# First mixer: the modulation rows of groups 2 and 3 weighted and added up on GpSimd

## The chip, the core and the metric

The kernel runs on one NeuronCore of a Trainium2 chip. The metric is the device time of one execution in microseconds (us). A NeuronCore has five engines with instruction queues of their own: TensorE (PE, matrix products into PSUM banks), VectorE (DVE), ScalarE (ACT), GpSimd (POOL) and SyncE (SP, which here only issues DMAs). They are ordered among one another by semaphores alone.

## What is computed

The reference is a two-layer transformer-like model on 512 tokens of width 1024, with a second block behind it. The change lies in the first layer's conditioning and its mixer:

```python
def _adaln(cvec, w_mod, b_mod, n_chunks):
    m = jax.nn.silu(cvec) @ w_mod[:, :n_chunks * D_MODEL] + b_mod[:n_chunks * D_MODEL]
    return [m[:, None, j * D_MODEL:(j + 1) * D_MODEL] for j in range(n_chunks)]

def _even_mixer(h, p, h0):
    proj = h @ p['w_in']
    ...
    hs, h_last = _rglru(xa_raw, p, h0)
    y_a = jax.nn.gelu(gate) * (hs[0] + jnp.flip(hs[1], axis=1)).astype(h.dtype)
    u = _dwconv1d(hy, p['conv_b_w'], p['conv_b_b'])
    v, *gates = jnp.split(u, HYENA_ORDER + 1, axis=-1)
    kf = _hyena_filters_fft(h.shape[1], p)
    z = v
    for o in range(HYENA_ORDER):
        z = gates[o] * _fftconv(z, kf[:, o], p['filt_bias'][o])
    return jnp.concatenate([y_a, z], axis=-1) @ p['w_out'], h_last
```

`_adaln` is a product of one vector (1024 long) with a weight matrix of 1024 x 6144 for each layer, in float32. Each layer's result gives the shifts, scales and gates of its norms and residual additions.

## The kernel before

**Modulation rows.** The weight matrix `w_mod` is cut into rows: row n of a group g (g = n // 8, c = n % 8) is 128 of the 1024 input channels by 2048 output columns, 1 MB. Eight rows make a group; three groups make a layer. `adaln_sync` (L601) loads row n into one of the slots of a ring once row n minus the number of slots has been used. `adaln_tensor` (L616) multiplies it: four products with the 32-column stationary tile `cs[:, c, :]` (`cond`: column 0 the activated conditioning, column 1 that of the context, the rest zero), one for each 512 of the 2048 columns, into the four 32-partition strips of bank 4 or 5. The eight rows of a group accumulate there. Then DVE copies the bank to `mod_rows` (`rows_vector`, L655), PE turns it with four transposes (`turned_tensor`), and DVE adds the bias and writes `mods` (`mods_vector`, two operations). Groups 0 and 1 are used at the opening; groups 2 and 3 (rows 16 to 31) are spread over the mixer, with the two halves of the `residual` buffer as slots, which is free then; x itself is loaded into it again (`x.again`, L1270) when row 31 has been used.

**The mixer.** The input projection is 20 blocks of 128 output channels. A block is eight products 128x128 by 128x512 on PE (16 records in the trace) from a ring of two weight tiles `wring` (SP loads block n after block n-2's product). Blocks 0 to 3 go to the recurrence (RG-LRU), together with the context's; blocks 4 to 15 to the Hyena part; 16 to 19 are the gate. DVE does a depthwise convolution on each of blocks 0 to 15 straight from the bank (banks 6 and 7 in turn, so block n waits for the convolution of block n-2), and between these, unit by unit (`unit_vector`, L1074), the recurrence: 8 units (4 context, 4 main) x 2 directions, six or seven operations each over 256 or 512 elements, a scan among them. ACT does the units' sigmoids, exponentials and roots (`unit_scalar`). Then for each of two orders `o`: turns, spectra (`hyena_bins_tensor`), products with the filter's spectrum on DVE, the inverse transform (`hyena_back_tensor`), with blocks 16 to 19 between them. Last comes the output projection (`out_tensor`), whose first halves need the gated recurrence output (`gated_vector`, `ya3`), and the routing of the experts.

**Order.** Each engine's order is written out by hand in `mixer0_sync`, `mixer0_tensor`, `mixer0_vector` and `mixer0_scalar`. The rows of groups 2 and 3 are generators there: `next(rows)` issues one row. On PE they stand behind blocks 5, 7, 9, 11, 13, 14, 15 (`ROWS_BEHIND`) and between the steps of the two orders; on SP they stand behind the load of the block that `ROWS_WITH` names. GpSimd has only the experts' six indirect DMAs, from 707 us on. `Mixer` lays out SBUF by hand: `lru_slots`, `lru_tmp` and `w_more` lie in a row, and behind them begins `spare`, the buffer of the first expert weight unit.

Of the kernel before, what the change touches and what calls it, by code (L numbers as in the profile page):

```python
# [9 lines left out]
ALU = mybir.AluOpType  # L10
# [3 lines left out]
P = 128  # L14
T = 512
D = 1024
KD = D // P
# [141 lines left out]
class Kernel:  # L159
# [52 lines left out]
    def act(self, ins, name=None):  # L212

        ins.then_inc(*self.up("scalar", name))
        self.nc.scalar.wait_ge(self.sems["scalar"], self.count["scalar"])

    def mm(self, out, lhsT, rhs, start=True, stop=True):
        return self.nc.tensor.matmul(out, lhsT, rhs, start=start, stop=stop, skip_group_check=True)  # L218
# [145 lines left out]
def all_steps(stream):  # L364
    for _ in stream:
        pass
# [232 lines left out]
NEARLY = 4 * KD  # L599
# [68 lines left out]
        k.vec(v.tensor_tensor(o, turned[:, :, :, r], bias, ALU.add), f"ad.mods{g}" if r else None)  # L668


def steps_of(n):

    for _ in range(n):
        yield
# [23 lines left out]
class Mixer:  # L698
    def __init__(self, k):
        at = Place(k.nc, k.base)  # L700
        self.kf = at.sb("spectrum", [P, 2, 9, RW])
        self.gw = at.sb("lru_w", [P, 16, P])
        self.filters = Filters(at.then())
        late = at.then()
        self.fw = late.sb("dft", [P, 2, 2 * T])
        self.inv = late.sb("idft", [P, 8, T // 2])
        self.pr = late.sb("proj", [P, 20, T])
        lru = late.then()
        self.slot = lru.sb("lru_slots", [P, 2, 2, 3, T])
        more = lru.then()  # L710
        self.tmp = lru.sb("lru_tmp", [P, 2, 2, T])
        self.we = lru.sb("w_more", [P, KD, P])
        hy = late.then()
        self.sd = hy.sb("z_spectrum", [P, 2, NT, RW])
        self.zt = hy.sb("z_tm", [P, 4, RW])
        self.xz = [self.pr[:, 0:KR, :].rearrange("p c (q t) -> p c q t", q=2), more.sb("z_halves", [P, KR, 2, T // 2])]
        k.mixed = lru.next
        top = Place(k.nc, (k.nc.sbuf_usable_end - 4 * (KD * TC + TC)) // 32 * 32)
        self.xc = top.sb("ctx", [P, KD, TC])
        self.rc = top.sb("ctx_rms", [P, TC])  # L720
        self.ra = k.SQ[:, :, :].rearrange("p s (c t) -> p (s c) t", c=2)
        self.wm = k.X[:, :, :].rearrange("p (s c) t -> p s (c t)", s=2)
# [463 lines left out]
def out_sync(k, m, experts):  # L1186

    p = k.nc.sync
    for i in range(KD):
        if i == 3:  # L1190
            p.wait_ge(*k.at("cc3.mm"))
            router_sync(k, experts)
            unit_sync(k, experts, 0)
            p.wait_ge(*k.at(f"hy1.product{NT - 1}"))
            for n in range(1, NEARLIER):
                unit_sync(k, experts, n)
        p.wait_ge(*k.at(f"in{18 + i}.mm" if i < 2 else "in19.mm" if i == 2 else f"wo.mm{i - 3}"))
        p.dma_start(out_weights(k, m, i % 3), k.blocks("w_out", i)).then_inc(*k.up(f"wo{i % 3}", f"wo.w{i}", 16))


def out_half_tensor(k, m, i, q):
    for c in range(4 * q, 4 * q + 4):
        ins = k.mm(k.bank[4 + i % 4][:, :], out_weights(k, m, i % 3)[:, c, :], m.pr[:, 4 + c, :], c == 0, c == KD - 1)
    return ins


def out_tensor(k, m, experts):
    t = k.nc.tensor
    for i in range(3):
        t.wait_ge(*k.at(f"wo.w{i}"))  # L1210
        t.wait_ge(*k.at("ya3"))
        out_half_tensor(k, m, i, 0)
    t.wait_ge(*k.at(f"hy1.out{KR - 1}"))
    for i in range(KD):
        if i >= 3:
            t.wait_ge(*k.at(f"wo.w{i}"))
            if i >= 4:
                t.wait_ge(*k.at(f"wo.out{i - 4}"))
            out_half_tensor(k, m, i, 0)
        out_half_tensor(k, m, i, 1).then_inc(*k.up("tensor", f"wo.mm{i}"))  # L1220
        if i:
            route_sums_tensor(k, experts, i - 1, k.H[:, i - 1, :])
    route_sums_tensor(k, experts, KD - 1, k.H[:, KD - 1, :])
# [13 lines left out]

ROWS_BEHIND = (5, 7, 9, 11, 13, 14, 15)  # L1240
ROWS_WITH = {7: 1, 9: 1, 11: 1, 13: 1, 15: 1, 16: 1, 17: 2, 18: 1}


def mixer0_sync(k, m, experts):
    p, a = k.nc.sync, k.a
    all_steps(adaln_sync(k, m.filters.wm, 0, KD))
    rows = adaln_sync(k, m.filters.wm, KD, 2 * KD, [f"ad.row{n}" for n in (6, 7, 5)])
    for _ in range(3):
        next(rows)
    p.wait_ge(*k.at("lru.clear"))  # L1250
    p.dma_start(m.gw[0:64, :, 0:64], a["lru_w"][0]).then_inc(*k.up("lru_w0", "lru.w0", 16))
    p.dma_start(m.gw[64:128, :, 64:128], a["lru_w"][1]).then_inc(*k.up("lru_w1", "lru.w1", 16))
    block_sync(k, 0)
    block_sync(k, 1)
    all_steps(rows)
    p.wait_ge(*k.at(f"ad.row{2 * KD - 1}"))
    p.dma_start(m.fw[:, :, :], a["dft"].rearrange("p (k t) -> p k t", k=2)).then_inc(*k.up("dft", "hy.dft", 16))
    p.dma_start(m.inv[:, :, :], a["idft"].rearrange("p (k t) -> p k t", k=8)).then_inc(*k.up("idft", "hy.idft", 16))
    rows = adaln_sync(k, m.wm, 2 * KD, NEARLY)
    p.wait_ge(*k.at(f"mx.scaled{KD - 1}"))  # L1260
    next(rows)
    next(rows)
    p.dma_start(k.C[:, NFIRST:], a["consts"][:, NFIRST:]).then_inc(*k.up("consts_more", "consts.more", 16))
    for n in range(2, 20):
        block_sync(k, n)
        for _ in range(ROWS_WITH.get(n, 0)):
            next(rows)
    all_steps(rows)
    p.wait_ge(*k.at(f"ad.row{NEARLY - 1}"))
    p.dma_start(k.X[:, :, :], a["x_fm"].rearrange("p (k t) -> p k t", k=KD)).then_inc(*k.up("x_in", "x.again", 16))  # L1270
    out_sync(k, m, experts)


def mixer0_tensor(k, m, experts):
    t = k.nc.tensor
    first = adaln_tensor(k, m.filters.wm, k.cs, 0, KD, k.mrow)
    second = adaln_tensor(k, m.filters.wm, k.cs, KD, 2 * KD, k.mrow)
    opening_tensor(k, m, m.filters, first, second)
    t.wait_ge(*k.at(f"mx.shifted{KD - 1}"))
    t.wait_ge(*k.at("lru.w0"))  # L1280
    t.wait_ge(*k.at("lru.w1"))
    rows = adaln_tensor(k, m.wm, k.cs, 2 * KD, NEARLY, k.mrow)
    for n in range(KR):
        ctx_block_tensor(k, m, n)
        block_tensor(k, n, 7, f"cx.conv{n - 1}" if n else "sp.row1")
        if n == 1:
            all_steps(bins_tensor(k, m.filters, 1))
        if n:
            unit_tensor(k, m, n - 1)
        else:  # L1290
            all_steps(second)
    for n in range(KR, 16):
        block_tensor(k, n, 6 + n % 2, f"in{n - 2}.out" if n >= 6 else "cc.conv3" if n == 4 else "cx.conv3")
        if n in UNIT_AFTER:
            unit_tensor(k, m, UNIT_AFTER[n])
        if n in ROWS_BEHIND:
            next(rows)
    for o in range(2):
        hyena_turn_tensor(k, m, o)
        next(rows, None)  # L1300
        block_tensor(k, 16 + 2 * o, 6, f"in{14 + 2 * o}.out")
        next(rows, None)
        hyena_bins_tensor(k, m, o)
        next(rows, None)
        block_tensor(k, 17 + 2 * o, 7, f"in{15 + 2 * o}.out")
        next(rows, None)
        hyena_back_tensor(k, m, o)
        next(rows, None)
    out_tensor(k, m, experts)
    t.wait_ge(*k.at("consts.more"))  # L1310
    fence(k, "layer0", "tensor")


def mixer0_vector(k, m, experts):
    v = k.nc.vector
    opening_vector(k, m, m.filters)
    rows_vector(k, 1, k.mrow)
    rows = adaln_vector(k, 2 * KD, NEARLY)
    for n in range(KR):
        v.wait_ge(*k.at(f"cc{n}.mm"))  # L1320
        dwconv_vector(k, m.ra[:, n, :], k.bank[6][:, 0:TC], TC, "conv_a_w", n, KR, 4, 1, "conv_a_b", n,
# [9 lines left out]
    for n in range(KR, 16):  # L1331
        v.wait_ge(*k.at(f"in{n}.mm"))
        c = n - KR
        dwconv_vector(k, m.pr[:, 8 + c, :], k.bank[6 + n % 2][:, :], T, "conv_b_w", c, 12, 3, 1, "conv_b_b", c, f"in{n}.out")
        if c < KR:
            folded_vector(k, m, 0, c)
        for u, d in chains.get(n, ()):
            unit_vector(k, m, u, d)
        if n in ROWS_BEHIND:
            next(rows)  # L1340
    next(rows)
    next(rows)
    hyena_products_vector(k, m, 0)
    next(rows)
    next(rows)
    for c in range(KR):
        hyena_out_vector(k, m, 0, c)
        folded_vector(k, m, 1, c)
    hyena_products_vector(k, m, 1)
    all_steps(rows)  # L1350
    for c in range(KR):
        gated_vector(k, m, c)
    for c in range(KR):
        hyena_out_vector(k, m, 1, c)
    out_vector(k, m, experts)
# [82 lines left out]
def router_sync(k, m):  # L1438
    k.nc.sync.dma_start(m.rt[:, :, :], k.a["router"][m.layer].rearrange("p (k e) -> p k e", k=KD)).then_inc(
        *k.up("router", f"{m.name}.router", 16))  # L1440
# [2168 lines left out]
def build(nc, a, known):  # L3609
    k = Kernel(nc, a, known)  # L3610
# [29 lines left out]
    experts_tensor(k, experts1, both_sums)  # L3640
    second_tensor(k, second)

    for m in (experts0, experts1):
        rows_pool(k, m)

# [108 lines left out]
```

## Time and profile before

| | us |
|---|---|
| Runs (3) | 2416.41, 2422.7, 2425.77 |
| Median | 2422.7 |
| Span of the profiled execution | 2423.9 |

One execution was taken by the hardware profiler. The profile's page gives the busy time of each engine, and behind it stands the trace, from which other views are drawn: groups of instructions by line (L612 is line 612 of the kernel) and shape, instructions in order of time with the idle time before them and what ended it, tables of stretches, the DMA issues, and the chain of work that ended last, followed back from the last instruction. All times count from the span's start. An operand form such as `bank<-residual,cond 128*32 128x512` is a product of a 128x32 stationary tile with 128x512 moving elements. A float32 product shows as two records. A record's end on PE is modelled, so the distance between starts is the better measure of its cost. The first mixer takes up roughly the first 435 us of the span.

### The profile page before, as it was taken

What the parts mean: (1) busy time and instruction counts of PE and PEld (TensorE: products, weight loads), DVE (VectorE), ACT (ScalarE), POOL (GpSimd) and SP (SyncE); (2) the same over time, 40 slices, a digit from 0 to 9 for tenths busy, and PEclk for the clock granted to TensorE, in tenths of its full rate; (3) what the DMA queues carried; (4) which work ended last, traced back from release to release, by engine and by line L of the source; (5) the groups of instructions that cost most, each with busy time, mean ns of one, the idle gap of its engine ahead of it and who ended that gap; (6) DMA issues with size and microseconds to landing.
All of it is one profiled execution on the core that took longest, in us unless ns stands there. A gap on an engine that the chain in (4) does not pass through costs nothing.

```text
span 2423.9 us, 30345 instructions
## 1 busy us (share of the span) xinstructions
PE 2263.7 (93%) x12864; PEld 1173.2 (48%) x12864; DVE 988.5 (41%) x1786; ACT 489.0 (20%) x881; POOL 6.0 (0%) x10
## 2 busy tenths in 40 slices
PE   8999999799999998988899999899999999998797
PEld 2454454444443333436544433337884447776445
DVE  6568543311112115675211111136752446545574
ACT  3275000211111102022111111111113321114501
POOL 0000000000000000000000000000000000000000
PEclk9999999899999999999999999999999999999899
DMA  8513434799999994562899999962222220221051
GB/s 310 212 52 113 164 123 174 308 411 428 428 427 427 427 394 156 217 253 103 370 410 427 428 427 427 427 270 72 87 87 56 82 71 21 68 97 63 35 191 70
DMA packets 72243, 564.32 MB, mean 233 GB/s; under 512 B 10825, under 2 KB 11337, under 8 KB 39403
## 3 DMA queue, kind: packets, MB, share of 16 engines
q1 hardware_dynamic: 63648, 538.76, 55.5%
q10 hardware_dynamic: 7596, 20.47, 2.2%
q0 software_dynamic: 864, 3.15, 0.3%
q8 instruction: 102, 1.67, 0.3%
q14 instruction: 33, 0.27, 0.0%
HBM read 547.67 MB, written 14.68 MB: 232 GB/s over the span
## 4 chain that ended last, share of the span: by engine, by line
PE 74%; DVE 12%; DMA 9%; ACT 3%; issue 2%; SPq 0%; ACTq 0%; DVEq 0%
PE bank L218 72%; DMA experts<-in_exp_w 7%; DMA fast_w<-in_w_in 2%; PE bank L221 1%; DVE wring L1578 0%; DVE max L1577 0%; ACT scores_t L3370 0%; DVE residual L1735 0%; DVE fast_s L2107 0%; DVE fast_s L2110 0%; DVE fast_s L2108 0%; DVE fast_s L2109 0%; ACT wring L1673 0%; DVE squares L1703 0%; DVE residual L523 0%
## 5 line engine op out<-in xcount | busy, mean ns | idle before, releaser
L218 PE MATMUL bank<-normed,wring 128*128 128x512 f32 (+2 forms) x1120 | 460.4, 591 | 3.9 <-ACT normed L1918 2.1
L218 PE MATMUL bank<-experts,wring 128*64 128x512 f32 x1632 | 361.1, 596 | 10.1 <-DMA experts<-in_exp_w 10.1
L218 PEld LDWEIGHTS bank<-normed,wring 128*128 128x128 f32 (+1 forms) x1120 | 190.6, 184 | 232.9 <-issue 226.1
L1703 DVE TENSOR_TENSOR squares<-squares,bank 128x512 f32<-128x512 f32 x32 | 22.0, 688 | 670.5 <-ACT squares L1697 670.5
L218 PEld LDWEIGHTS bank<-experts,wring 128*64 128x64 f32 x1632 | 116.9, 137 | 247.4 <-issue 229.9
L218 PE MATMUL bank<-experts,hs_t 128*64 128x512 f32 x768 | 183.5, 598 | 9.3 <-DMA experts<-in_exp_w 8.9
L218 PE MATMUL bank<-rms,y 128*128 128x512 f32 x256 | 125.5, 609 | 6.0 <-ACT y L1829 2.7
L1735 DVE SCALAR_TENSOR_TENSOR residual<-bank,mods,residual 128x512 f32<-128x512 f32 x128 | 96.1, 751 | 74.1 <-PE bank L218 67.4
L218 PEld LDWEIGHTS bank<-experts,hs_t 128*64 128x64 f32 x768 | 61.4, 138 | 124.7 <-issue 122.8
L1697 ACT ACTIVATE squares<-bank 128x512 f32<-128x512 f32 x32 | 19.1, 598 | 469.9 <-PE bank L218 469.9
L218 PE MATMUL bank<-proj 64*64 64x64 f32 (+1 forms) x2192 | 94.0, 233 | 5.8 <-ACT proj L2927 4.8
L218 PEld LDWEIGHTS bank<-proj 64*64 64x64 f32 (+1 forms) x2192 | 77.5, 139 | 16.4 <-issue 5.6
L1673 ACT ACTIVATE wring<-bank,mods,gains 128x128 f32<-128x128 f32 x128 | 58.6, 458 | 103.7 <-PE bank L218 90.9
L218 PE MATMUL bank<-fast_t,fast_s 128*128 128x256 f32 x336 | 74.8, 379 | 0.0
L218 PE MATMUL bank<-proj,wring 128*128 128x512 f32 (+1 forms) x168 | 69.3, 565 | 5.5 <-DVE proj L1362 3.9
L218 PE MATMUL bank<-normed,hs_t 128*64 128x512 f32 x160 | 70.5, 594 | 1.8 <-ACT wring L1673 0.9
L218 PEld LDWEIGHTS bank<-rms,y 128*128 128x128 f32 x256 | 42.8, 190 | 52.7 <-DVE residual L1735 25.9
L218 PEld LDWEIGHTS bank<-fast_t,fast_s 128*128 128x128 f32 x336 | 63.8, 190 | 8.7
L218 PE MATMUL bank<-normed,fast_w 128*128 128x256 f32 (+1 forms) x256 | 66.7, 406 | 0.0
L218 PEld LDWEIGHTS bank<-pick,h_tm 128*128 128x128 f32 x512 | 59.4, 192 | 5.7 <-issue 4.3
L1829 ACT COPY y<-bank 128x512 f32<-128x512 f32 x32 | 18.8, 586 | 211.7 <-PE bank L218 211.2
L218 PE MATMUL bank<-pick,h_tm 128*128 128x128 f32 x512 | 59.8, 275 | 0.0
(616 smaller groups left out, 2756.0 us busy)
## 6 DMA issues: line engine op xcount, KB each, us to landing
experts<-in_exp_w SPq DMA_DIRECT2D x146, 2048.0 KB, 22.4
spare<-in_exp_w SPq DMA_DIRECT2D x20, 2048.0 KB, 22.7
normed<-in_exp_w SPq DMA_DIRECT2D x20, 2048.0 KB, 23.3
wring<-in_w_in SPq DMA_DIRECT2D x44, 512.0 KB, 3.6
wmod<-in_w_mod SPq DMA_DIRECT2D x16, 1024.0 KB, 5.9
residual<-in_w_mod SPq DMA_DIRECT2D x16, 1024.0 KB, 6.3
cf_wmod<-in_w_mod SPq DMA_DIRECT2D x16, 1024.0 KB, 5.7
fast_w<-in_w_in SPq DMA_DIRECT2D x30, 512.0 KB, 4.3
```

Source lines behind the costliest of these rows:

```text
L218: return self.nc.tensor.matmul(out, lhsT, rhs, start=start, stop=stop, skip_group_check=True)
L221: return self.nc.tensor.transpose(out, in_, self.con("ident", 0, n, 0, n))
L1673: k.act(k.nc.scalar.activation(m.xs[:, c, :], k.bank[6 + h][:, (c % 4) * P:(c % 4 + 1) * P], ACT.Identity, bias=k.MOD[:, m.layer, 24 + c, ...
L1697: k.act(k.nc.scalar.activation(m.hs[:, e, :], k.bank[2 - 2 * e][:, :], ACT.Silu), f"{m.name}.silu{i}.{e}")
L1703: k.vec(v.tensor_tensor(m.hs[:, e, :], m.hs[:, e, :], k.bank[3 - 2 * e][:, :], ALU.mult), f"{m.name}.hs{i}.{e}")
L1735: k.vec(v.scalar_tensor_tensor(out=k.X[:, c, :], in0=k.bank[4 + c % 2][:, :], scalar=k.MOD[:, m.layer, 40 + c, 0:1], in1=k.X[:, c, :], op0 ...
L1829: k.act(s.copy(m.yy[:, 512 * f:512 * f + 512], k.bank[f][:, :]), f"{m.name}.yy{i}.{f}")
```

## The change

On GpSimd a new function, `summed_pool`, takes each row of groups 2 and 3 as it lands: it multiplies the 128x2048 row with its channel's conditioning (column 0 of `cond`, one scalar for each partition) in place and adds it to an accumulator `mod_sums`; the first row of a group is multiplied straight into it. When a group's eight rows are in, PE multiplies the accumulator once with a 128x32 tile of ones (four products, one for each strip), which adds up over the partitions, and the copy, the turns and the addition of the bias follow as before. The bias is added for column 0 only (`gain_mods_vector`). The sums and turns of group 2 stand behind blocks 10 and 12, those of group 3 behind blocks 18 and 19, and the gate products on DVE now stand before the addition of group 3's bias. SP issues one row with each of blocks 2 to 9 and 12 to 17. The accumulator takes 8 KB a partition where `spare` begins, so SP waits for the sums of group 3 before the first expert unit. The output projection waits for `ad.mods3`, since it writes bank 5.

```diff
@@ class Kernel
+    def pool(self, ins, name=None):
+        ins.then_inc(*self.up("pool", name))
+        self.nc.gpsimd.wait_ge(self.sems["pool"], self.count["pool"])
@@ new functions
+def summed_pool(k, m, lo, hi):
+    p = k.nc.gpsimd
+    for n in range(lo, hi):
+        g, c = n // KD, n % KD
+        w, scale = m.wm[:, (n - lo) % 2, :], k.cs[:, c, 0:1]
+        p.wait_ge(*k.at(f"ad.w{n}"))
+        if c == 0:
+            p.wait_ge(*k.at(f"ad.sums{g - 1}" if n > lo else "cond"))
+            k.pool(p.tensor_scalar(m.acc[:, :], w, scale, None, ALU.mult), f"ad.row{n}")
+        else:
+            k.pool(p.tensor_scalar(w, w, scale, None, ALU.mult))
+            k.pool(p.tensor_tensor(m.acc[:, :], m.acc[:, :], w, ALU.add), f"ad.row{n}")
+
+def sums_tensor(k, m, g):
+    t = k.nc.tensor
+    t.wait_ge(*k.at(f"ad.row{KD * g + KD - 1}"))
+    t.wait_ge(*k.at(f"ad.mods{g - 2}"))
+    for q in range(4):
+        ins = k.mm(k.bank[4 + g % 2][32 * q:32 * q + 32, :], k.con("ones", 0, 32), m.acc[:, 512 * q:512 * q + 512])
+    ins.then_inc(*k.up("tensor", f"ad.sums{g}"))
+
+def sums_vector(k, g, rows):
+    k.nc.vector.wait_ge(*k.at(f"ad.sums{g}"))
+    k.vec(k.nc.vector.tensor_copy(rows[:, :], k.bank[4 + g % 2][:, :]), f"ad.rows{g}")
+
+def gain_mods_vector(k, g):
...
+    k.vec(v.tensor_tensor(o, turned[:, :, :, 0], bias, ALU.add), f"ad.mods{g}")
@@ class Mixer
         hy = late.then()
+        self.acc = lru.then().sb("mod_sums", [P, 2048])
@@ def out_sync
             router_sync(k, experts)
+            p.wait_ge(*k.at(f"ad.sums{NEARLY // KD - 1}"))
             unit_sync(k, experts, 0)
@@ def out_tensor
         t.wait_ge(*k.at("ya3"))
+        t.wait_ge(*k.at("ad.mods3"))
         out_half_tensor(k, m, i, 0)
@@
-ROWS_BEHIND = (5, 7, 9, 11, 13, 14, 15)
-ROWS_WITH = {7: 1, 9: 1, 11: 1, 13: 1, 15: 1, 16: 1, 17: 2, 18: 1}
+ROWS_WITH = (*range(2, 10), *range(12, 18))
@@ def mixer0_sync
         block_sync(k, n)
-        for _ in range(ROWS_WITH.get(n, 0)):
+        if n in ROWS_WITH:
             next(rows)
-    all_steps(rows)
@@ def mixer0_tensor
-    rows = adaln_tensor(k, m.wm, k.cs, 2 * KD, NEARLY, k.mrow)
...
-        if n in ROWS_BEHIND:
-            next(rows)
+        if n == 10:
+            sums_tensor(k, m, 2)
+        if n == 12:
+            turned_tensor(k, 2, k.mrow)
     for o in range(2):
         hyena_turn_tensor(k, m, o)
-        next(rows, None)
         block_tensor(k, 16 + 2 * o, 6, f"in{14 + 2 * o}.out")
-        next(rows, None)
+        if o:
+            sums_tensor(k, m, 3)
         hyena_bins_tensor(k, m, o)
-        next(rows, None)
         block_tensor(k, 17 + 2 * o, 7, f"in{15 + 2 * o}.out")
-        next(rows, None)
+        if o:
+            turned_tensor(k, 3, k.mrow)
         hyena_back_tensor(k, m, o)
-        next(rows, None)
@@ def mixer0_vector
-        if n in ROWS_BEHIND:
-            next(rows)
-    next(rows)
-    next(rows)
+        if n == 11:
+            sums_vector(k, 2, k.mrow)
+        if n == 13:
+            gain_mods_vector(k, 2)
     hyena_products_vector(k, m, 0)
-    next(rows)
-    next(rows)
...
     hyena_products_vector(k, m, 1)
-    all_steps(rows)
+    sums_vector(k, 3, k.mrow)
     for c in range(KR):
         gated_vector(k, m, c)
+    gain_mods_vector(k, 3)
@@ def build
+    summed_pool(k, mixer0, 2 * KD, NEARLY)
     for m in (experts0, experts1):
         rows_pool(k, m)
```

## Rows read from the trace of the kernel before

**Rows 1.** The page, part 1: busy time, share of the span and instructions of each engine.

```profile
PE 2263.7 (93%) x12864; PEld 1173.2 (48%) x12864; DVE 988.5 (41%) x1786; ACT 489.0 (20%) x881; POOL 6.0 (0%) x10
```

**Rows 2.** Table of stretches; columns named in its first line.

```profile
core 0: us, PE busy (x) PEld busy (x) DVE busy (x) ACT busy (x) POOL busy (x), PEclk, DMA share, GB/s
...
172.00:261.00 89.00, 89.00 (x252) 36.69 (x251) 70.97 (x105) 42.99 (x52) 0.00 (x0) 1.00 0.37 128
261.00:370.00 109.00, 99.53 (x361) 53.16 (x359) 51.98 (x88) 9.85 (x15) 0.00 (x0) 0.98 0.40 155
```

**Rows 3.** Chain of work that ended last, 90 to 520 us: start, length, what.

```profile
128.00 132.07 PE bank L218 x376
...
283.49 16.42 PE bank L218 x56
...
369.27 0.70 DVE proj L1362
...
370.11 62.91 PE bank L218 x226
```

**Rows 4.** PE in order of time, 168 to 392 us; then the rows' products by tile.

```profile
191.24 1.07 PE L218 MATMUL bank<-residual,cond 128*32 128x512 f32 x8
192.24 7.13 PE L218 MATMUL bank<-normed,wring 128*128 128x512 f32 x16
...
310.18 1.06 PE L218 MATMUL bank<-residual,cond 128*32 128x512 f32 x8
313.54 2.79 PE L221 MATMUL bank<-consts,z_halves 128*128 128x128 f32 x16 [2.29 <-DVE proj L1176]
...
318.03 0.66 PE L221 MATMUL bank<-consts,mod_rows 128*128 128x128 f32 x4
...
365.62 0.60 PE L221 MATMUL bank<-consts,mod_rows 128*128 128x128 f32 x4
...
L218 PE MATMUL bank<-residual,cond x128: 592/617/1059, 172.9 to 351.2; 128*32 128x512 f32 x128
```

**Rows 5.** Groups of instructions by line and shape, DVE, 140 to 262 us.

```profile
L559 DVE SCALAR_TENSOR_TENSOR proj<-bank,vecs,proj 128x511 f32<-128x511 f32 x28 | 21.0, 750 | 1.0
L554 DVE TENSOR_SCALAR proj<-bank,vecs 128x512 f32<-128x512 f32 x14 | 11.3, 810 | 20.2 <-PE bank L218 20.0
...
L1084 DVE TENSOR_TENSOR lru_slots<-lru_slots 128x512 f32<-128x512 f32 x8 | 5.5, 692 | 0.3
L1089 DVE TENSOR_TENSOR_SCAN lru_slots<-lru_slots,lru_state 128x512 f32<-128x512 f32 x4 | 5.1, 1284 | 0.1
...
L1082 DVE TENSOR_SCALAR lru_slots<-lru_slots 128x512 f32<-128x512 f32 x8 | 3.4, 427 | 0.3
...
L1084 DVE TENSOR_TENSOR lru_slots<-lru_slots 128x256 f32<-128x256 f32 x8 | 3.4, 425 | 0.3
...
L1089 DVE TENSOR_TENSOR_SCAN lru_slots<-lru_slots 128x256 f32<-128x256 f32 x4 | 2.8, 691 | 0.1
L1082 DVE TENSOR_SCALAR lru_slots<-lru_slots 128x256 f32<-128x256 f32 x8 | 2.4, 294 | 0.3
```

**Rows 6.** Instructions in order of time, DVE, 250 to 280 us.

```profile
259.19 0.81 DVE L554 TENSOR_SCALAR proj<-bank,vecs 128x512 f32<-128x512 f32 x1 [5.67 <-PE bank L218]
...
274.77 0.69 DVE L1147 TENSOR_TENSOR squares<-bank,spectrum 128x512 f32<-128x512 f32 x1 [10.97 <-PE bank L218]
...
276.22 0.69 DVE L1149 TENSOR_TENSOR z_spectrum<-squares 128x512 f32<-128x512 f32 x1
```

**Rows 7.** Groups of instructions by line, POOL, whole span (the memsets' other three are alike).

```profile
L1650 POOL DMA_INDIRECT h_tm<-token_rows,place x6 | 5.8, 959 | 1511.7 <-DVE gate L1624 1302.9 <-DVE gate L1622 208.8
L3750 POOL MEMSET const-uint8-127<- 128x1 uint8 x1 | 0.1, 118 | 0.0
```

**Rows 8.** DMA issues, 80 to 520 us (last number: median us to landing); SP's timeline.

```profile
residual<-in_w_mod SPq DMA_DIRECT2D x16, 1024.0 KB, 6.3
...
351.83 0.33 SPq L1270 DMA_DIRECT2D residual<-in_x_fm  x1
```

More of the change, by code:

```diff
@@ L668, in mods_vector @@
         k.vec(v.tensor_tensor(o, turned[:, :, :, r], bias, ALU.add), f"ad.mods{g}" if r else None)
+def summed_pool(k, m, lo, hi):
[21 more added lines that the diff above has]
+def gain_mods_vector(k, g):
+    v, layer, i = k.nc.vector, g // 3, g % 3
+    v.wait_ge(*k.at(f"ad.turned{g}"))
+    turned = k.bank[4 + g % 2][:, :].rearrange("p (j q r) -> p q j r", q=4, r=32)
+    bias = k.vector_of("b_mod", 48 * layer + 16 * i, 16).rearrange("p (q j) -> p q j", q=4)
+    o = k.MOD[:, layer, 16 * i:16 * i + 16, 0].rearrange("p (q j) -> p q j", q=4)
+    k.vec(v.tensor_tensor(o, turned[:, :, :, 0], bias, ALU.add), f"ad.mods{g}")
 def steps_of(n):
@@ L1317, in mixer0_vector @@
     rows_vector(k, 1, k.mrow)
-    rows = adaln_vector(k, 2 * KD, NEARLY)
     for n in range(KR):
```

## Prediction

> **What bounds the kernel now.** I read the page first. TensorE (PE) is busy for 93% of the span, VectorE (DVE) for 41%, GpSimd (POOL) for 6.0 us in all [rows 1]. The edit touches one stage only, the first mixer from 88 to 370 us, so the averages say little, and the second view is the table of stretches. From 172 to 261 us PE is busy for 89.00 of 89 us at full clock, and DVE for 70.97 us; from 261 to 370 us PE has 9.5 us of idle time [rows 2]. The third is the chain of work that ended last. It runs on PE without a break from 128.00 to 260.1 us, later for 16.42 us up to 299.9, and ends the stage with DVE's four gate products, the last at 369.27 us, after which PE goes on at 370.11 [rows 3]. So a microsecond of PE work taken out before 261 us shortens the kernel, as long as DVE, which is busy for 80% there, still keeps up. PE has two banks for the blocks, and block n waits for DVE's convolution of block n-2.
>
> **What is removed from TensorE.** A row is four column groups, and its eight records together take 1.07 us; the next block starts 1.00 us after the row (191.24 to 192.24) [rows 4]. I count 1.0 us for each. The record says 16 rows x 8 = 128 [rows 4]. Nine rows lie before the spectra of order 0 at 271 us: 9.0 us, less 1.0 for the new sums of group 2 (four products of the same shape as a row) and 0.6 for its four turns, moved here from 318.03 us, where they took 0.66 [rows 4]: 7.4 us gained. Of the seven others, the two behind the spectra and block 17 give 2.0. The one at 310.18 gives nothing: PE then waits until 313.54 for DVE in any case [rows 4]. The next, with the turns of group 2 behind it at 318.03, gives 1.0 + 0.6 = 1.6. The one behind block 18 is replaced by the sums of group 3: 0. The last two give 2.0 less 0.6 for the turns of group 3, moved ahead of the inverse transform: 1.4. The sum so far is 7.4 + 2.0 + 1.6 + 1.4 = 12.4 us.
>
> **What moves at the end of the stage.** Now the turns (0.60 us) come behind the inverse transform, then DVE's two additions and four gate products, and PE stands still from 366.22 to 370.11, 3.89 us, before the output projection [rows 3, 4]. Afterwards the gate products wait only for block 19's activation and lie beside the 14 us inverse transform, and the last turns are over before it. PE goes on at once: 0.6 + 3.9 = 4.5 us gained. What is late next there is DVE's second output step, which now begins with the first finished column chunk instead of at 370 us; three half projections of 3.5 us each (half a block's 7.0) lie before PE needs it, so nothing of the 4.5 comes back. The new wait for `ad.mods3` in front of the projection is the last of those short DVE operations and is met. Altogether TensorE's side gives 12.4 + 4.5 = 16.9 us, taken as 17. Everything behind (router, experts' weight loads) starts from events of this stage and shifts with it.
>
> **What is added to GpSimd.** There are 2 + 14 x 2 = 30 instructions over 128x2048 floats. The trace has no arithmetic on POOL, only four memsets of 128x1 at about 0.1 us and six indirect DMAs [rows 7], so both ends come from DVE. A two-input operation there takes 425 ns for 256 elements and 692 for 512, 1.04 ns an element; for 2048 that is 0.69 + 1536 x 1.04 ns = 2.3 us. The scan takes 2.31 ns an element (1284 - 692 over 256), 4.8 us for 2048. One input in SBUF takes 294 and 427 ns, 0.52 ns an element: 1.2 us, or 2.4 us without that double rate [rows 5]. I take 4.5 us for the addition, two operands fetched one after the other at DVE's pace of 1.04 ns, plus issue, near the upper end, and 2.0 for the scaling: 6.5 us a row, 3.5 to 7.2. The Trainium skill (GPSIMD Engine Reference, 3.1 Elementwise) gives 4497 ns for that addition; no trace here shows it.
>
> **Its schedule.** A row lands 6.3 us after its issue [rows 8]. Each buffer is used in turn, so two rows take at least 6.3 + 6.5 = 12.8 us, 6.4 a row, and GpSimd's own time is 6.5, against 7.0 us for a bare block [rows 4] and about 8.5 with what stands behind it (blocks 8 to 15 take 68 us, from 191.24 to 259.2 [rows 4, 6]). GpSimd keeps up: group 2 is added up by about 183 us, and its sums stand behind block 10 at about 215. Row 24 must wait for these sums, since there is one accumulator, and from there rows follow block by block until about 268 us; the sums of group 3 are wanted at about 312. On SP's queue each row's wait now stands in front of the next weight block. Row n-2 is done before that block may be fetched, so at 6.5 us it costs nothing. The copy of x, the output weights and the experts' first units stand behind row 31 as they did (x at 351.83 [rows 8]); they go out earlier. The wait for `ad.sums3` ahead of unit 0 is met by order, being behind block 19's product. DVE loses two small additions. Behind GpSimd's rows only the experts' indirect DMAs are queued, which come long after [rows 7].
>
> **What it may cost DVE.** This decides. From 140 to 262 us DVE runs the recurrence: its operations take two tensors from SBUF (692 ns for 512 elements). The spectra products show the same 0.69 us with one operand from PSUM as with both from SBUF, and one SBUF input runs at twice the rate of a PSUM one, 427 against 810 ns [rows 5, 6]. So DVE draws on SBUF over two read paths at once. The question is whether GpSimd comes in over one of these. Bounds: nothing, or DVE's two-input operations stand for the whole GpSimd instruction. I take the upper end, because DVE's rows need both paths in full and leave no cycle to share. Rows 16 to 19 are done before 140 us, where DVE has little to do. Rows 20 to 30, eleven of them, fall beside the recurrence. In each DVE loses 6.5 us less what it can do with one SBUF operand. That is the convolution, 0.81 + 2 x 0.75 = 2.3 us [rows 5], beside every second row: 1.2. So 11 x 5.3 = 58 us. DVE's idle time in front of the block convolutions is 20 us in this stretch [rows 5], 5.67 of it at 259.19 us [rows 6]. 58 - 20 = 38 us come through to PE, which stands at blocks 7, 8 and 12 to 16 for a convolution that DVE has not reached. Net: -17 + 38 = +21 us. PE's new idle time may also lower its clock; the stretch that has such idle time is at 0.98 [rows 2], about 2 us in 109, and it stays out.
>
> What the rows show is two read paths; that GpSimd sits on one of them they can't. The Trainium skill says so (SBUF: State Buffer, Practical consequences): a Vector instruction with two SBUF inputs contends with a GpSimd instruction that reads SBUF, and the pair is held for a whole instruction. By that rule it is the +21 us sum, without it the -17 us one. Its advice for such a pair is to schedule whichever is off the critical path, which speaks against this change, where the lent engine takes the path of a busy one.
>
> **The rivals.** (a) GpSimd reads beside DVE at no cost. For it: nothing in the trace shows a conflict, and there are sixteen rows with ample slack before either sum is wanted. Against: the two read paths above. Mechanism and place: fewer than the 20 us of DVE's idle time are lost, that is under 1.8 us a row, and the 14 products and the 3.9 us wait go. Time: 2422.7 - 17 = 2406; it decides for faster. (b) They share path by path: DVE goes at half speed for the 11 x 6.5 = 71 us, loses 35, 20 of it idle: -17 + 15 = -2 us, 2421. (c) The path is free but GpSimd is slower than all rows suggest, say 13 us a row. Against 8.5 us a block that is 4.5 too slow, and behind rows 26 to 29 SP holds back four blocks' weights: 4 x 4.5 = 18 us, -17 + 18 = +1 us, 2424; it begins to cost at 8.5 us a row.
>
> **How the numbers follow.** The profiled span is 2423.9 us and the median of the runs 2422.7, 1.2 less, so I add to the median: 2422.7 + 21 = 2444. The likeliest case's own range comes from the price of a row: with 3.5 us, 11 x 2.3 = 25, less 20, is 5, giving -12; with 7.2 us and nothing done beside it, 79 - 20 - 17 = +42: 2411 to 2465. Chances: blocking 0.50 (0.46 slower, 0.04 within), free 0.34 (0.31 faster, 0.03 within), shared 0.11 (within), slow GpSimd 0.05 (within). About 0.5%, 12 us, is what a measurement can tell from no change. Faster 0.31, same 0.23, slower 0.46. The range takes in (a): 2404 to 2462.
>
> **What would show it.** In the profile after: 30 POOL instructions, near 2.0 and 4.5 us. Blocking shows in DVE's recurrence operations: some of 692 ns stretched to several us while POOL is busy, and PE idle in front of blocks, released by DVE's convolution. If these stay at 692 ns, (a) holds, and PE's stretch to 261 us ends 8 us sooner with no gaps. Under (c) PE waits for the block weights' DMA. The gain at 366 to 370 us should be there in every case. I am wrong if DVE is barely slowed, or if GpSimd's rows fall mostly where DVE idles.

## The result and the profile after

The changed kernel is slower: 2464.4 us as the median of its runs (2461.2 to 2466.4), against 2422.3 for the kernel before in the same comparison. The ratio is 1.0175, 95% interval 1.016 to 1.019, which is +42 us. The forecast was slower, at +21 us, and its range ended at 2462. The profiled execution has a span of 2459.9 us, 36.0 more than that of before; it is the shortest of its runs.

The page of the changed kernel, part 1, beside [rows 1]:

```profile
PE 2246.5 (91%) x12752; PEld 1170.9 (48%) x12752; DVE 1059.0 (43%) x1784; ACT 488.7 (20%) x881; POOL 158.6 (6%) x40
```

TensorE is busy for 17 us less. The work taken out is 112 records, about 15 us at 1.07 us for eight [rows 4]; the rest mixes in other differences, among them blocks that run slower behind a wait (below). VectorE has 70.5 us more, although two of its instructions fewer are in the list (1784 against 1786), and GpSimd went from 6.0 to 158.6 us. DVE has been given no work: its instructions take longer. The table of stretches, beside [rows 2] (the same columns):

```profile
core 0: us, PE busy (x) PEld busy (x) DVE busy (x) ACT busy (x) POOL busy (x), PEclk, DMA share, GB/s
...
172.00:261.00 89.00, 69.37 (x163) 29.68 (x161) 85.27 (x94) 51.22 (x65) 39.13 (x8) 0.91 0.29 100
261.00:330.00 69.00, 41.36 (x100) 19.14 (x100) 57.79 (x39) 4.22 (x6) 58.32 (x12) 0.79 0.31 107
```

PE, which had filled 172 to 261 us without a gap, is busy for 69.37 of these 89 us; DVE is busy for 85.27 instead of 70.97. They have changed places. GpSimd's groups by line, beside [rows 7]:

```profile
L688 POOL TENSOR_SCALAR residual<-residual,cond 128x2048 f32<-128x2048 f32 x14 | 77.7, 5553 | 31.9 <-DMA residual<-in_w_mod 31.0
L689 POOL TENSOR_TENSOR mod_sums<-mod_sums,residual 128x2048 f32<-128x2048 f32 x14 | 63.9, 4563 | 1.2
```

The addition took 4.56 us on average (I had taken 4.5), the weighting 5.55 (I had taken 2.0). PE in order of time, with what ended its idle time in brackets, beside [rows 4]:

```profile
158.04 9.80 PE L223 MATMUL bank<-normed,wring 128*128 128x512 f32 x16 [6.44 <-DVE squares L564]
...
200.99 5.38 PE L223 MATMUL bank<-proj,lru_w 128*128 128x512 f32 x8 [14.26 <-DVE lru_slots L1128]
...
280.54 1.08 PE L226 MATMUL bank<-consts,mod_rows 128*128 128x128 f32 x4 [24.92 <-DVE mod_rows L704]
...
310.54 8.65 PE L223 MATMUL bank<-normed,wring 128*128 128x512 f32 x16 [4.16 <-DVE proj L564]
...
330.56 8.83 PE L223 MATMUL bank<-z_tm,dft 128*128 128x512 f32 x16 [4.51 <-DVE z_spectrum L1199]
...
396.47 13.98 PE L223 MATMUL bank<-idft,z_spectrum 128*128 128x256 f32 x64
410.29 7.03 PE L223 MATMUL bank<-proj,wring 128*128 128x512 f32 x16
```

In the kernel before PE was busy without a gap from 128.00 us until the products of order 0. Now it stands still for 6.44, 14.26, 24.92 and 4.16 us, each time for DVE, and for 4.51 us between the spectra of order 0, where it was 1.04. Only the 6.44 and the 4.16 us lie in front of a block (4 and 16). The 14.26 us lie in front of the products of a recurrence unit, and the 24.92 us between block 12 and the turns of group 2, which wait for DVE's copy. The end of the stage is as predicted: the output projection at 410.29 follows the inverse transform (396.47 + 13.98 = 410.45, its end being modelled) with no gap, where there were 3.89 us.

### The profile page after: what moved, and what is told of

It is laid out like the page before. It is cut to its first block, busy times and chain, and to the rows that moved or that the text cites. A ratio compares the mean times of both kernels' runs of the same rounds, so it can differ in the third digit from the quotient of the medians.

```text
span 2459.9 us, 30167 instructions
## 1 busy us (share of the span) xinstructions
PE 2246.5 (91%) x12752; PEld 1170.9 (48%) x12752; DVE 1059.0 (43%) x1784; ACT 488.7 (20%) x881; POOL 158.6 (6%) x40
## 4 chain that ended last, share of the span: by engine, by line
PE 69%; DVE 17%; DMA 9%; ACT 3%; issue 2%; ACTq 0%; SPq 0%; DVEq 0%
PE bank L223 67%; DMA experts<-in_exp_w 6%; DMA fast_w<-in_w_in 2%; PE bank L226 1%; DVE lru_slots L1130 1%; DMA ctx<-in_ctx_fm 1%; DVE proj L564 1%; DVE lru_slots L1131 1%; DVE lru_slots L1129 1%; DVE lru_slots L1128 1%; DVE wring L1623 0%; DVE lru_slots L1127 0%; DVE max L1622 0%; ACT scores_t L3415 0%; DVE residual L1780 0%
## 5 line engine op out<-in xcount | busy, mean ns | idle before, releaser
L223 PE MATMUL bank<-normed,wring 128*128 128x512 f32 (+2 forms) x1120 | 466.0, 598 | 14.5 <-DVE squares L564 6.4
L1695 POOL DMA_INDIRECT h_tm<-token_rows,place x6 | 5.8, 971 | 1221.2 <-PE bank L223 597.7
L688 POOL TENSOR_SCALAR residual<-residual,cond 128x2048 f32<-128x2048 f32 x14 | 77.7, 5553 | 31.9 <-DMA residual<-in_w_mod 31.0
L223 PE MATMUL bank<-normed,hs_t 128*64 128x512 f32 x160 | 70.5, 594 | 1.8 <-ACT wring L1718 0.9
L689 POOL TENSOR_TENSOR mod_sums<-mod_sums,residual 128x2048 f32<-128x2048 f32 x14 | 63.9, 4563 | 1.2
```

What stands on the lines that cost most here:

```text
L688: k.pool(p.tensor_scalar(w, w, scale, None, ALU.mult))
L689: k.pool(p.tensor_tensor(m.acc[:, :], m.acc[:, :], w, ALU.add), f"ad.row{n}")
```

## The mechanism, instruction by instruction

Two stretches of the changed kernel side by side, GpSimd first, then DVE. They are lined up by their starts:

```profile
241.92 5.56 POOL L686 TENSOR_SCALAR mod_sums<-residual,cond 128x2048 f32<-128x2048 f32 x1 [47.31 <-PE bank L223]
247.57 5.48 POOL L688 TENSOR_SCALAR residual<-residual,cond 128x2048 f32<-128x2048 f32 x1
...
264.15 4.54 POOL L689 TENSOR_TENSOR mod_sums<-mod_sums,residual 128x2048 f32<-128x2048 f32 x1
...
241.48 0.69 DVE L1128 SCALAR_TENSOR_TENSOR lru_slots<-lru_tmp,lru_slots 128x512 f32<-128x512 f32 x1
242.21 5.55 DVE L1129 TENSOR_SCALAR lru_slots<-lru_slots 128x512 f32<-128x512 f32 x1
247.80 4.08 DVE L1130 TENSOR_TENSOR lru_slots<-lru_slots,proj 128x512 f32<-128x512 f32 x1
251.91 0.69 DVE L1131 TENSOR_TENSOR lru_slots<-lru_slots 128x512 f32<-128x512 f32 x1
...
264.38 4.86 DVE L1130 TENSOR_TENSOR lru_slots<-lru_slots,proj 128x512 f32<-128x512 f32 x1
```

DVE's `TENSOR_SCALAR` at 242.21, SBUF to SBUF, took 0.43 us before [rows 5]; it now takes 5.55 and ends at 247.76. Less its own 0.43 that is 247.33, just when GpSimd's weighting ends (241.92 + 5.56 = 247.48). The next weighting begins at 247.57, and DVE's `TENSOR_TENSOR` with two operands in SBUF (0.69 us before) takes 4.08: less its own 0.69 it was let go at 251.19. The one at 251.91 takes 0.69 again, though GpSimd's instruction lasts until 253.05. So a two-input operation is held for the first 3.6 us of a weighting of 5.48, one at the double rate for all of it. In this trace eight two-input operations meet a weighting in its first part, and all are let go 3.6 to 3.9 us after its recorded start. Beside an addition (264.15 to 268.69) the two-input operation takes 4.86 us; less its own 0.69 that is 268.55, the addition's end. The operation just ahead at 241.48 lasts 0.69 us as ever, though GpSimd began within it: it was already on its way. All convolution steps, with one operand in a bank and one in SBUF, keep their 750 ns:

```profile
L1130 DVE TENSOR_TENSOR lru_slots<-lru_slots,proj 128x512 f32<-128x512 f32 x8 | 17.3, 2158 | 0.3
L564 DVE SCALAR_TENSOR_TENSOR proj<-bank,vecs,proj 128x511 f32<-128x511 f32 x23 | 17.2, 750 | 0.8
...
L1129 DVE TENSOR_SCALAR lru_slots<-lru_slots 128x512 f32<-128x512 f32 x8 | 9.8, 1228 | 0.3
```

(Groups of DVE by line and shape, 140 to 300 us, beside [rows 5].) The Trainium skill (SBUF — State Buffer, Who interferes with whom, Practical consequences) has this rule: VectorE with two SBUF inputs contends with a GpSimd instruction that reads SBUF, and with any GpSimd instruction when it runs in a 2-port mode, as the double-rate operations would. The traces agree in who waits and who doesn't. In how long they differ for one case: its summary says that the second one blocks until the first finishes, and here a two-input operation is let through after 3.6 of the weighting's 5.48 us. Why, no run here shows.

## Experiments

### The order alone, without GpSimd's work

```diff
-            k.pool(p.tensor_scalar(m.acc[:, :], w, scale, None, ALU.mult), f"ad.row{n}")
+            k.pool(p.memset(m.acc[:, :], 0.0), f"ad.row{n}")
         else:
-            k.pool(p.tensor_scalar(w, w, scale, None, ALU.mult))
-            k.pool(p.tensor_tensor(m.acc[:, :], m.acc[:, :], w, ALU.add), f"ad.row{n}")
+            k.pool(p.tensor_scalar(w[:, 0:1], w[:, 0:1], scale, None, ALU.mult))
+            k.pool(p.tensor_tensor(m.acc[:, 0:1], m.acc[:, 0:1], w[:, 0:1], ALU.add), f"ad.row{n}")
```

> The changed kernel in all its order and waits, but GpSimd's work is left out: the accumulator is set to 0 once a group, and of each later row only one column of 2048 is weighted and added, so the sums of groups 2 and 3 aren't computed. Theory A (DVE is held up by GpSimd's instructions): PE's side of the change alone is left, 17 us under the kernel before, about 2406 us, and DVE's recurrence operations are back at 692 ns. Theory B (the new order, with PE's sums and turns waiting for DVE's copy in the middle of the recurrence, and the gate products moved, costs the time by itself): it stays above the kernel before, 2430 us or more. Theory C (GpSimd too slow for SP's queue) also gives 2406.

Measured: 2402.3 us, ratio 0.9932 (0.9913 to 0.9951), which is -16.5 us (interval -21 to -12). The edit's gain on TensorE, -17 by the forecast, is there, and the order, the waits and the place of the turns cost nothing while DVE keeps up. Between 125 and 269 us PE waits for DVE once, 1.91 us ahead of the turns of group 2. Theory B falls. DVE is busy for 989.6 us:

```profile
PE 2237.8 (93%) x12752; PEld 1169.3 (49%) x12752; DVE 989.6 (41%) x1784; ACT 488.9 (20%) x881; POOL 21.1 (1%) x40
```

(page of this kernel, part 1). So GpSimd's work costs 42.4 + 16.5 = 59 us (each term known to about 4 us), and it stretches DVE's instructions by 1059.0 - 989.6 = 69.4 us.

### Weighting alone and addition alone

```diff
-            k.pool(p.tensor_tensor(m.acc[:, :], m.acc[:, :], w, ALU.add), f"ad.row{n}")
+            k.pool(p.tensor_tensor(m.acc[:, 0:1], m.acc[:, 0:1], w[:, 0:1], ALU.add), f"ad.row{n}")
```

> The changed kernel with the weighting of all 16 rows in full (5.5 us each), but the addition only in one column of 2048, so the sums are incomplete. Theory A: DVE is held up by the weighting alone, 11 rows x (4.1 - 1.2) = 32 us, 20 of them idle time that DVE has, less 17: -5 us, about 2417 us; DVE operations are stretched by up to about 4 us. Theory C (SP's queue held back by 10.1 us a row): at 5.5 us a row nothing is held back, 2406 us, and DVE's operations stay at 692 ns.

Measured: 2427.0 us, ratio 1.0025 (1.0011 to 1.0040), +6 us; DVE is busy for 1019.9 us, 30.3 more than in e1_no_pool_work. The other way round, the weighting of rows 1 to 7 of a group cut down to one column and the addition in full:

> The changed kernel with the addition of rows in full (4.5 us each), the weighting of rows 1 to 7 of a group only in one column of 2048, so the sums are those of unweighted rows. Theory A: 11 x (4.5 - 1.2) = 36 us, less 20 idle, less 17: about -1 us, 2421 us. Theory C: 2406 us. If the addition (two operands read) holds DVE up and the weighting (one operand) doesn't, this one is near 2440 and the weighting alone near 2406.

Measured: 2431.9 us, ratio 1.0048 (1.0033 to 1.0063), +12 us; DVE is busy for 1022.2 us, 32.6 more. Theory C wanted 2406 from both and falls: at 4.7 or 5.5 us a row nothing is held back on SP's queue, and both still lose the gain. Either instruction holds DVE up, with one operand read from SBUF as with two. Both came out 10 us above my estimate; I had let 20 us of the loss fall into idle time. From e1_no_pool_work's -16.5 they have lost 22.6 and 28.1 us, so only 30.3 - 22.6 = 8 and 32.6 - 28.1 = 5 us were hidden.

### Busy, but only writing

```diff
-            k.pool(p.tensor_scalar(w, w, scale, None, ALU.mult))
+            for _ in range(5):
+                k.pool(p.memset(w, 0.0))
```

with the addition cut down to one column and the first row replaced by a fill, as in e1_no_pool_work.

> The changed kernel, in which GpSimd fills each landed row with zeros five times (a fill of 128x2048 took 1.81 us in e1_no_pool_work, so about 9 us a row and 10 with the small operations) instead of weighting and adding it; the sums are not computed. GpSimd is as busy as in the changed kernel (10.1 us a row) but reads nothing large from SBUF. Theory A1 (the read path is what is held): DVE's operations stay at 692 ns, and the time is 2402 us as in e1_no_pool_work. Theory A2 (writing holds DVE up as well): near 2460 us. Theory C (a slow GpSimd holds back the block weights on SP's queue): PE waits for DMAs of weights, 10.1 - 8.5 = 1.6 us for each of four to six blocks, 2406 to 2412 us, with DVE's operations at 692 ns.

Measured: 2403.1 us, ratio 0.9925 (0.9897 to 0.9953), although GpSimd is busy for 140.4 us. Its groups and then those of DVE, by line and shape:

```profile
L689 POOL MEMSET residual<- 128x2048 f32 x70 | 126.8, 1811 | 25.4 <-DMA residual<-in_w_mod 21.5
...
L1130 DVE TENSOR_SCALAR lru_slots<-lru_slots 128x256 f32<-128x256 f32 x8 | 7.5, 931 | 0.3
L1130 DVE TENSOR_SCALAR lru_slots<-lru_slots 128x512 f32<-128x512 f32 x8 | 6.7, 836 | 0.3
...
L1132 DVE TENSOR_TENSOR lru_slots<-lru_slots 128x512 f32<-128x512 f32 x8 | 5.5, 692 | 0.3
```

This kernel separates three things that the changed kernel has together. A GpSimd that is only busy costs nothing that shows. Nor does a row that takes 9.3 us before SP can go on: PE waits for the DMA of a weight block once, for 0.33 us. In the changed kernel, whose rows take 10.1 us, none of PE's waits between 128 and 410 us is for a DMA, so theory C falls. And writes don't hold up a two-input operation (692 ns). They do hold up the double-rate ones: 931 and 836 ns on average where it was 294 and 427, DVE busy by 7.1 us more, which its idle time hid. So it is GpSimd's reading that costs here.

### The price of the weighting

```diff
-            k.pool(p.tensor_scalar(w, w, scale, None, ALU.mult))
+            k.pool(p.tensor_scalar(w, w, 0.5, None, ALU.mult))
```

> The changed kernel with the weighting by a constant 0.5 instead of the per-partition scalar read from SBUF (the sums are therefore others). If the per-partition scalar makes the weighting cost 5.5 us instead of the 2.0 that I took, it falls to about 2 us and the time to about 2445 us, where I had predicted it. If the float32 scaling costs 5.5 us with either, the time stays at 2464 us.

Measured once: 2464.7 us. The group by line on GpSimd:

```profile
L688 POOL TENSOR_SCALAR residual<-residual 128x2048 f32<-128x2048 f32 x14 | 76.6, 5471 | 30.0 <-DMA residual<-in_w_mod 29.2
```

5.47 us, so the scalar operand isn't what makes it dear. Scaling 2048 floats in place costs GpSimd more than adding two such rows (4.5 us). Why, no run here shows.

### Where the turns stand

```diff
-        if n == 12:
+        if n == 15:
             turned_tensor(k, 2, k.mrow)
```

> The changed kernel with the turns of group 2 behind block 15 instead of block 12, and the addition of its bias behind the products of order 0. In the changed kernel PE stood still for 24.92 us in front of these turns. Theory A (DVE is the bound throughout the recurrence, and the wait only shows where PE meets it): the wait goes to the blocks behind, and the time stays within 5 us of 2464 us. Theory B (the position of the turns makes a wait of its own, since DVE copies the sums only behind a recurrence unit): 10 to 20 us less, 2444 to 2454 us.

Measured: 2467.1 us, ratio 1.019 (1.015 to 1.023), from two runs 13 us apart. PE in order of time, beside the changed kernel's 24.92 us in one piece:

```profile
256.32 7.11 PE L223 MATMUL bank<-normed,wring 128*128 128x512 f32 x16 [0.86 <-DVE proj L564]
282.81 8.88 PE L223 MATMUL bank<-normed,wring 128*128 128x512 f32 x16 [19.39 <-DVE proj L564]
298.02 9.80 PE L223 MATMUL bank<-normed,wring 128*128 128x512 f32 x16 [6.33 <-DVE proj L564]
...
316.30 9.20 PE L223 MATMUL bank<-normed,wring 128*128 128x512 f32 x16 [6.29 <-DVE proj L564]
```

The wait has broken up into 0.86, 19.39, 6.33 and 6.29 us ahead of blocks 13 to 16, each for a convolution: 32.9 us, where the changed kernel has 24.92 + 4.16 = 29.1 in this part. The gain of 10 to 20 us that theory B wanted is outside the interval. The turns only mark the point where PE met DVE; whether their place is worth a few us, two runs can't tell.

### Does the lower clock cost anything?

Behind its waits PE is slow: block 4 took 9.80 us where 7.03 is usual, and the stretch from 261 to 330 us has a granted clock of 0.79, a mean between the levels of 2.4 and 1.2 GHz. I counted about 10 us of longer blocks and formed theory D, that they are part of the 42. The test fills the waits with idle work:

```diff
+def warm_tensor(k, m, count):
+    for _ in range(count):
+        k.mm(k.bank[5][:, :], m.gw[:, 0, :], m.gw[:, 4:8, :].rearrange("p a b -> p (a b)"))
```

> The changed kernel with 53 products into a bank that nobody reads, put where PE stood still in it: 6 ahead of block 4, 14 behind block 6, 25 ahead of the turns of group 2, 4 behind the first turns and 4 ahead of the third spectrum of order 0, about 0.88 us each, no more in each place than the wait there. DVE's delays stay. Theory D (behind each wait PE works at a lower granted clock: block 4 took 9.80 us for 7.03, and the stretch 261 to 330 us was at 0.79): the slow stretches go, and it is up to 10 us faster than the changed kernel, about 2454 to 2458 us. If the clock cost nothing that counts, since DVE bounds the stretch anyway, it stays at 2464 us; if the products delay PE, it is above 2466 us.

Measured: 2466.3 us, ratio 1.0174 (1.0145 to 1.0203). The stretches:

```profile
125.00:172.00 47.00, 44.98 (x137) 25.50 (x137) 33.35 (x43) 26.41 (x40) 26.67 (x6) 1.00 0.27 101
172.00:261.00 89.00, 87.25 (x209) 37.78 (x208) 85.66 (x97) 51.60 (x65) 42.29 (x8) 1.00 0.30 107
261.00:330.00 69.00, 53.98 (x130) 24.32 (x129) 57.05 (x32) 4.22 (x6) 55.81 (x12) 0.88 0.25 91
```

The clock was back at 1.00 up to 261 us, blocks took 7.03 us there, and the time didn't fall. But this run by itself doesn't settle theory D, because DVE's delays didn't stay what they were, which I had expected them to. PE in its trace:

```profile
316.87 9.91 PE L223 MATMUL bank<-normed,wring 128*128 128x512 f32 x16 [11.13 <-DVE proj L564]
```

Block 16 waited for 11.13 us instead of 4.16 and was as slow as before. In the changed kernel GpSimd's row 29 begins at 297.18 us, and rows 29 and 30 hold two operations of the last recurrence unit; here row 29 begins at 292.99, and the two rows hold four. Up to block 16 DVE's operations were stretched by 72.7 us instead of 67.3.

What does settle it up to block 16 is DVE's idle time in the changed kernel. From 138 to 312 us it waits for PE once, for 0.54 us:

```profile
230.51 0.81 DVE L559 TENSOR_SCALAR proj<-bank,vecs 128x512 f32<-128x512 f32 x1 [0.54 <-PE bank L223]
```

DVE sets the pace there, and a PE at full clock couldn't have made it faster by more than that. Behind it PE is on the path again: block 16 took 8.65 us instead of 7.03, and the pair of spectra at 330.56 lost about 1 us. So theory D falls as to its 10 us, and about 2 to 3 us of the 42 may be the clock's; no run separates them.

### The move at the end alone

```diff
         next(rows, None)
+        if o:
+            next(rows, None)
         block_tensor(k, 17 + 2 * o, 7, f"in{15 + 2 * o}.out")
         next(rows, None)
         hyena_back_tensor(k, m, o)
-        next(rows, None)
+        if not o:
+            next(rows, None)
@@ def out_tensor
         t.wait_ge(*k.at("ya3"))
+        t.wait_ge(*k.at("ad.mods3"))
@@ def mixer0_vector
-    all_steps(rows)
+    for _ in range(5):
+        next(rows)
     for c in range(KR):
         gated_vector(k, m, c)
+    all_steps(rows)
```

so rows 30 and 31 both stand ahead of block 19.

> The kernel before with nothing but the move at the end: all rows stay on TensorE, rows 30 and 31 both ahead of block 19, the last turns behind it and ahead of the inverse transform, the gate products ahead of the last addition of the bias. By my sum the 3.9 us wait and the 0.6 us of turns behind the inverse transform go, while the turns now come ahead of it (0.6): -3.9 us, about 2415.5 us beside 2419.2. If the end of the stage is set by something else (the output weights, DVE's output step), it stays within 1 us.

Measured: 2414.7 us, ratio 0.9970 (0.9955 to 0.9984), -4 to -11 us; the sum of -3.9 lies at the edge of the interval. The traces are narrower: from the first products of the mixer (126.88 us here, 128.00 before) to the output projection it is 237.6 us instead of 242.1, so 4.5 us. The projection follows the inverse transform at once:

```profile
350.26 0.60 PE L221 MATMUL bank<-consts,mod_rows 128*128 128x128 f32 x4
350.70 13.98 PE L218 MATMUL bank<-idft,z_spectrum 128*128 128x256 f32 x64
364.51 7.03 PE L218 MATMUL bank<-proj,wring 128*128 128x512 f32 x16
```

(PE in order of time, beside the gap of 3.89 us in [rows 4] and [rows 3]).

### The same sums on VectorE, where it was idle

```diff
+def summed_vector(k, m, *which):
+    v = k.nc.vector
+    for n in which:
+        g, c = n // KD, n % KD
+        w, scale = m.wm[:, n % 2, :], k.cs[:, c, 0:1]
...
+            k.vec(v.scalar_tensor_tensor(out=m.acc[:, :], in0=w, scalar=scale, in1=m.acc[:, :], op0=ALU.mult, op1=ALU.add),
+                  f"ad.row{n}")
-ROWS_WITH = (*range(2, 10), *range(12, 18))
+ROWS_WITH = {2: 1, 3: 5, 5: 1, 6: 1, 10: 1, 12: 1, 14: 1, 17: 3}
@@ def mixer0_vector
+        if n == 1:
+            summed_vector(k, m, *range(16, 22))
...
+        summed_vector(k, m, *{6: (24,), 8: (25,), 10: (26,), 14: (27, 28), 15: (29, 30)}.get(n, ()))
     hyena_products_vector(k, m, 0)
+    summed_vector(k, m, 31)
```

with the sums of group 2 behind block 5 and its turns behind block 10.

> The changed kernel with the 16 rows weighted and added up on DVE, one two-input operation a row, where DVE was idle in the kernel before: rows 16 to 21 behind block 1, 22 and 23 ahead of block 2's convolution, 24, 25 and 26 in idle times of the recurrence, 27 to 30 behind the convolutions of blocks 14 and 15, row 31 behind the products of order 0. By the slope of 1.04 ns an element an operation takes 2.3 us, 36 us in all, against 22 + 5 + 8 + 16 + 8 = 59 us of idle time at these places. Theory A: GpSimd does nothing, DVE's recurrence operations stay at 692 ns, and all of PE's 17 us come through as in e1_no_pool_work: 2402 us, up to 2407 if the three rows inside the recurrence delay a block. If the rows add to DVE's path after all, above 2410 us.

Measured: 2400.3 us, ratio 0.9912 (0.9890 to 0.9935), -21 us: faster than both kernels. The instructions of the tile `mod_sums`, and PE where the only waits from 125 to 275 us stand:

```profile
L704 DVE SCALAR_TENSOR_TENSOR mod_sums<-residual,cond,mod_sums x14: 2350/2352/2353, 109.7 to 280.4; 128x2048 f32<-128x2048 f32 x14
L702 DVE TENSOR_SCALAR mod_sums<-residual,cond x2: 1287/1288/1289, 108.4 to 186.0; 128x2048 f32<-128x2048 f32 x2
...
124.85 1.97 PE L223 MATMUL bank<-squares,lru_w 128*128 128x256 f32 x8 [0.81 <-ACT spectrum L1059]
...
267.38 3.70 PE L223 MATMUL bank<-z_tm,dft 128*128 128x512 f32 x8 [1.50 <-DVE z_spectrum L1215]
271.74 3.70 PE L223 MATMUL bank<-z_tm,dft 128*128 128x512 f32 x8 [0.65 <-DVE z_spectrum L1215]
```

14 x 2.35 + 2 x 1.29 = 35.5 us of DVE's own time. That is half of the 69.4 us that GpSimd's help took from it. Because it is placed where DVE waited anyway, PE has no new wait; the one at 267.38 is 1.50 us, where there was 1.05. Two things differ from the changed kernel at once, the engine and the places. Rows 16 to 19 cost nothing on GpSimd either, where DVE had little to do, and no run puts all of GpSimd's rows at such places, so this run doesn't show that the engine alone makes the difference.

## Why the prediction was right in kind and short in size

Two terms of the sum -17 + 58 - 20 = +21 failed, by about 10 us each: DVE's loss of 58 us, which was 69, and the 20 us of idle time set against it, which were under 10.

**TensorE's side: right.** The sum was -17 us; with GpSimd's work taken out it is -16.5, within an interval of -21 to -12. The end of the stage gives 4.5 us alone, against 3.9 by the sum, and its wait is gone in the changed kernel too.

**Who is held up: right.** DVE's two-input operations wait for GpSimd's instructions, and PE waits for DVE. The bound "for the whole GpSimd instruction" holds for the addition and for double-rate operations; for two-input ones beside a weighting it is 3.6 of 5.5 us. The places were mostly wrong: I had PE standing at blocks 7, 8 and 12 to 16 for convolutions, and 39 of its 54 us of waits lie in front of a unit's products and of the turns. Rival (a), free reading at -17 us, and rival (b), half speed at -2 us, are out by the stretched operations and the time. Rival (c), SP's queue, is out by the kernel that only writes, and because PE waits for no DMA.

**The price of a row: wrong, the first half of the miss.** I took the weighting at 2.0 us, between DVE's rows of 1.2 and 2.4 [rows 5]. It took 5.5, above the upper end. A row was 10.1 us on GpSimd instead of 6.5, and outside the range of 3.5 to 7.2. DVE's own price for one operand said nothing about GpSimd's.

**The share that DVE loses: too high, which covered part of this.** I let DVE lose 5.3 of 6.5 us a row, 82%, over eleven rows; at 10.1 us a row that share would have made 91 us. It lost 69.4. Summed up by operation in the trace, rows 20 to 29 took 67.3 of the 97 us that GpSimd worked on them, since a weighting lets two-input operations go early and convolutions aren't held. Row 30 met only convolutions and cost nothing, and row 31, which I hadn't counted, held a product of order 0 for 3.5 us. (That makes 70.8; e1_no_pool_work has 1.3 us of this too, where its fill holds one operation.)

**The idle time of DVE: wrong, the other half.** I set the 20 us of idle time of the kernel before against the loss. Part of it was there because PE was slower, and it is this change that makes PE faster. Another part lay ahead of the first row that falls beside the recurrence. The group of DVE's convolutions in e1_no_pool_work, 137 to 255 us, beside the 20.2 us in [rows 5]:

```profile
L559 DVE TENSOR_SCALAR proj<-bank,vecs 128x512 f32<-128x512 f32 x14 | 11.3, 811 | 14.5 <-PE bank L223 14.2
```

It is 14.5 us: 5.7 us are gone, which I had counted twice, once as gain on PE and once as room on DVE. Of the 14.5, 4.77 lie ahead of row 20, as in the kernel before, and were never room for it: 9.7 us are left. The changed kernel used up all but 0.5 of them. The corrected sum is -16.5 + 69.4 - 9.7 = +43 us, and measured were +42. It is put together after the fact from terms known to about 4 us, so that it meets the time within 1 us is partly luck. With one instruction alone less was hidden (8 and 5 us), and the traces agree in kind: behind the start of row 20 DVE's waits for PE still added up to 2.8 us with the weighting alone and 7.1 with the addition alone, of 9.5 in e1_no_pool_work.

**The clock: nearly right to leave out, for another reason.** I left it out as small. It fell to 0.79 in a stretch of 69 us. Up to block 16 that cost nothing, because DVE was the bound; behind it, 2 to 3 us at most.

**The range.** Its likeliest case reached to +42, but the whole range stopped at 2462, 3 us below that case's own upper end of 2465. That end met the measured time by other terms than the true ones: 7.2 us a row all lost, and 20 us hidden. With the row's price unseen in the trace, the upper end should have been the wider one.

## What to carry to other kernels

An engine that looks free may still hold up its neighbour. Before lending GpSimd work beside VectorE, count VectorE's operations in that stretch that read two tensors from SBUF or run at the double rate, and charge each GpSimd instruction that meets one with up to its whole length (67 of 97 us here). Do that count in the kernel as it will be: idle time that exists because the bound engine was slow goes away with the same change that makes it faster, and idle time ahead of the new work is no room for it. Where the receiving work is short on the busy engine (2.35 us for a fused multiply and add, against 10.1 on the free one), placing it in that engine's own gaps can beat moving it away.

## What the runs showed of the hardware

- GpSimd's scaling of 128x2048 floats in place took 5.44 to 5.76 us and its addition 4.49 to 5.07; a fill of that size 1.81. DVE took 2.35 for multiply and add fused, and 1.29 for scaling alone. I had not expected the one-operand operation to be the dearer one on GpSimd.
- Holding goes both ways: GpSimd's addition at 253.14 us took 5.07 us instead of 4.50 with DVE's scan running into it until 253.91.
- GpSimd's writes alone hold DVE's double-rate operations (427 to 836 ns) but not its two-input ones (692 ns).
- Keeping PE busy through its waits brought the granted clock from 0.91 back to 1.00 (172 to 261 us); the time stayed (ratio 1.0174 against 1.0175). DVE set the pace there, and in this run it was held a little longer.
